# A second layer's modulation vectors computed by GpSimd products and ScalarE row sums instead of TensorE matmuls

## What is computed

```python
def modulation(cond, w, b):                       # w is 1024 x 3072
    m = jax.nn.silu(cond) @ w + b
    return jnp.split(m, 3, axis=-1)

for l in range(DEPTH):                            # DEPTH = 2
    sh, sc, gt = modulation(c, ada_w[l], ada_b[l])
    shc, scc, gtc = modulation(c_ctx, ada_w[l], ada_b[l])
    h  = rms_norm(x,  norm_pre[l]) * (1.0 + sc[:, None]) + sh[:, None]
    hc = rms_norm(xc, norm_pre[l]) * (1.0 + scc) + shc
    ...
```

## Time and profile before

| what | value |
|---|---|
| median of 3 runs | 2044.37 us |
| the profiled execution | 2042.73 us, span 2040.9 us, mean granted clock 0.986 |
| TensorE matmul busy | 1960.0 us (96%) |
| VectorE busy | 1296.8 us (64%) |
| ScalarE busy | 978.1 us (48%) |
| GpSimd busy | 30.3 us (1%), 23 instructions |
| DMA | 351.84 MB, mean 172 GB/s |

### The profile page before, as it was taken

How to read it: one execution, slowest core, us unless ns; L and a number is a source line. 1 busy time by engine, 2 the same in 40 slices (tenths; PEclk the granted TensorE clock), 3 DMA queues, 4 the chain that set the end, 5 groups by cost and what they waited for, 6 DMA issues and landing times.

```text
span 2040.9 us, 29528 instructions
## 1 busy us (share of the span) xinstructions
PE 1960.0 (96%) x12558; PEld 1702.9 (83%) x12558; DVE 1296.8 (64%) x1748; ACT 978.1 (48%) x1457; POOL 30.3 (1%) x23
## 2 busy tenths in 40 slices
PE   7799999999999999999989999999999999989998
PEld 3699999899888889999878887678888888768887
DVE  3877756878645778865565565755557555676555
ACT  1355445465334546534454445554445444565444
POOL 1300000000000000000000000000000000000000
PEclk8899999999999999999999999999999999999999
DMA  7544555434676533455445554355555555525554
GB/s 307 194 155 145 163 180 170 149 125 135 212 252 229 195 128 129 144 188 181 161 140 191 186 166 161 109 167 189 189 175 178 193 186 186 176 73 176 186 187 143
DMA packets 95410, 351.84 MB, mean 172 GB/s; under 512 B 10608, under 2 KB 10736, under 8 KB 94768
## 3 DMA queue, kind: packets, MB, share of 16 engines
q1 hardware_dynamic: 94032, 341.08, 50.6%
q0 software_dynamic: 960, 7.37, 0.9%
q10 hardware_dynamic: 288, 1.51, 0.2%
HBM read 348.87 MB, written 1.05 MB: 171 GB/s over the span
## 4 chain that ended last, share of the span: by engine, by line
PE 83%; DVE 11%; ACT 3%; DMA 2%; issue 1%; SPq 0%; DVEq 0%; ACTq 0%
PE PS L551 25%; PE PS L553 24%; PE PS L552 24%; DVE w_lo L1805 3%; DMA raw<-weights 2%; ACT w_hi L1293 1%; PE PS L629 1%; PE PS L723 1%; PE PS L954 1%; PE PS L742 1%; PE PS L917 1%; PE PS L1036 1%; PE PS L806 1%; PE PS L732 0%; PE PS L1047 0%
## 5 line engine op out<-in xcount | busy, mean ns | idle before, releaser
L1805 DVE TENSOR_TENSOR w_lo<-raw,w_hi 128x1024 fp32r<-128x1024 f32 x600 | 733.2, 1232 | 400.4 <-ACT w_hi L1293 399.0
L1293 ACT ACTIVATE w_hi<-raw 128x1024 fp32r<-128x1024 f32 x600 | 624.8, 1055 | 409.4 <-DMA raw<-weights 404.7
L551 PE MATMUL PS<-h_hi,w_hi 128*128 128x256 f32 x1568 | 455.3, 290 | 14.5 <-DVE h_lo L1823 5.4
L552 PE MATMUL PS<-h_lo,w_hi 128*128 128x256 f32 x1568 | 445.2, 284 | 0.0
L553 PE MATMUL PS<-h_hi,w_lo 128*128 128x256 f32 x1568 | 445.1, 284 | 0.0
L551 PE MATMUL PS<-w_hi,h_hi 128*128 128x512 f32 (+1 forms) x1024 | 389.2, 380 | 8.7 <-DVE h_lo L2171 6.5
L553 PE MATMUL PS<-w_hi,h_lo 128*128 128x512 f32 (+1 forms) x1024 | 380.7, 372 | 0.0
L552 PE MATMUL PS<-w_lo,h_hi 128*128 128x512 f32 (+1 forms) x1024 | 379.4, 370 | 0.0
L551 PEld LDWEIGHTS PS<-h_hi,w_hi 128*128 128x128 f32 x1568 | 302.1, 193 | 33.1 <-issue 18.9
L552 PEld LDWEIGHTS PS<-h_lo,w_hi 128*128 128x128 f32 x1568 | 302.4, 193 | 0.6 <-issue 0.5
L553 PEld LDWEIGHTS PS<-h_hi,w_lo 128*128 128x128 f32 x1568 | 302.2, 193 | 0.0
(11 more groups left out here) (256 smaller groups left out, 1855.0 us busy)
## 6 DMA issues: line engine op xcount, KB each, us to landing
raw<-weights SPq DMA_DIRECT2D x642, 512.0 KB, 3.4
x<-weights SPq DMA_DIRECT2D x6, 512.0 KB, 10.2
layer<-layer_in POOLq DMA_DIRECT2D x2, 1536.0 KB, 11.4
cx<-ctx_in POOLq DMA_DIRECT2D x1, 1024.0 KB, 8.5
x<-x_in POOLq DMA_DIRECT2D x1, 1024.0 KB, 12.5
out<-arena SPq DMA_DIRECT2D x4, 256.0 KB, 2.0
consts<-consts_in POOLq DMA_DIRECT2D x1, 928.0 KB, 9.2
arena<-filter_consts_in ACTq DMA_DIRECT2D x1, 896.0 KB, 8.3
```

The source lines that it names most:

```text
L551: pe.matmul(dst, hi, m_hi_, start=first, stop=False, **kw)
L552: pe.matmul(dst, hi, m_lo_, start=False, stop=False, **kw)
L1293: nc.scalar.activation(w_hi[:, r, :], raw[:, r, :], ACT.Copy).then_inc(w_hi_ready, 1)
L1805: V.tensor_tensor(w_lo[:, r, :], raw[:, r, :], f32(w_hi[:, r, :]), ALU.subtract).then_inc(w_lo_ready, 1)
```

## The change

- Layer 1's modulation leaves TensorE, PSUM and the ring. Its weights lie in DRAM transposed, a slot holding 128 output columns on the partitions and their 1024 weights along the row.
- A new input `cond_in` holds both condition vectors, copied to all 128 partitions (1 MB). GpSimd's queue loads it, ScalarE applies SiLU to it (`cond_silu`, behind the splits of `keys_queries`' last projection pair), and this happens twice, once in pass 0 and once in pass 1, because the memory (`beside`, in `g_hi` and `g_lo`) is used by each pass's merge stage.
- For each of the 24 slots GpSimd's queue loads the weights into one of two buffers, GpSimd makes two products of 128 x 1024 (weights by the token row, weights by the context row), and ScalarE sums each product along its row (`ada_row`: a Copy with an accumulator). There are two product buffers: a product waits until the row before last was summed.
- Pass 0's attention takes 8 slots (16 products, 2 row sums a step), pass 1's takes 16 (32 products, 4 row sums a step). The row sums stand right behind `take_turned` in each step.
- Pass 1's merge stage becomes like that of passes 0 and 2: 36 slots, no `ada`, no `ada_turn`, no copies of rows.
- VectorE's first write of `g_hi` in each of the two passes waits for the pass's row sums; `mod_vectors(1)` waits for all of them.

```diff
+            def load_ada(n):
+                pool.dma_start(ada_w[:, n % 2, :], weights[dram_pass[1] - ADA_SLOTS + n]).then_inc(ada_w_loaded[n % 2], 16)
+
+            def modulation_rows(part_):
+
+                first, end = ADA_ENDS[part_], ADA_ENDS[part_ + 1]
+                pool.wait_ge(spec_pair, DEPTH)
+                pool.dma_start(cond_rows[:, :, :], cond_in).then_inc(cond_loaded, 16)
+                load_ada(first)
+                load_ada(first + 1)
+
+                def product(i):
+                    n, w = divmod(i, 2)
+                    if i >= 2:
+                        pool.wait_ge(ada_sum, i - 1)
+                    nc.gpsimd.tensor_tensor(ada_prod[:, w, :], ada_w[:, n % 2, :], cond_rows[:, w, :],
+                                            ALU.mult).then_inc(ada_prod_ready, 1)
+
+                for n in range(first, end):
+                    if n == first:
+                        pool.wait_ge(cond_rows_act, part_ + 1)
+                    pool.wait_ge(ada_w_loaded[n % 2], 16 * (n // 2 + 1))
+                    product(2 * n)
+                    product(2 * n + 1)
+                    if n + 2 < end:
+                        pool.wait_ge(ada_prod_ready, 2 * n + 2)
+                        load_ada(n + 2)
+
+            modulation_rows(0)
+            pool.wait_ge(w_used, start["pass1"])
+            modulation_rows(1)
...
-                        if p == 1:
-                            ada(c, b, 0, i)
-                            c += 1
...
+            def cond_silu(part_):
+
+                act.wait_ge(cond_loaded, 16 * (part_ + 1))
+                nc.scalar.activation(cond_rows[:, :, :], cond_rows[:, :, :], ACT.Silu).then_inc(cond_rows_act, 1)
+
+            def ada_row(i):
+
+                act.wait_ge(ada_prod_ready, i + 1)
+                nc.scalar.activation(ada_prod[:, i % 2, :], ada_prod[:, i % 2, :], ACT.Copy,
+                                     accum_out=ada_sums[:, i:i + 1]).then_inc(ada_sum, 1)
...
                     splits(c0 + part["v"] + 2 + 2 * n)
                     take_turned(p, n)
+                    if p == 0:
+                        ada_rows_behind(p, 2 * n, 2 * n + 2)
+                    else:
+                        ada_rows_behind(p, 4 * n, 4 * n + 4)
...
+                    if p < 2 and (b, j) == (0, 0):
+                        dve.wait_ge(ada_sum, 2 * ADA_ENDS[p + 1])
```

More of the change, by code:

```diff
@@ L84, in places, with build @@
     return out, at
-def build(nc, weights, x_in, ctx_in, cols_in, consts_in, filter_consts_in, layer_in, filter_in, lam_in, tail_in, out):
+def build(nc, weights, x_in, ctx_in, cond_in, cols_in, consts_in, filter_consts_in, layer_in, filter_in, lam_in, tail_in, out):
     col_at, ncols = places(COLUMNS)
@@ L110, in build @@
     stretch("pass0", dram_pass[0], PASS_SLOTS)
[L111 to L113 removed]
+    stretch("pass1", dram_pass[0], PASS_SLOTS)
     stretch("ctx_k", dram_pass[1], 2)
@@ L118, in build @@
     dram = dram_pass[1] + PASS_SLOTS
-    for p in (0, 2):
+    for p in range(3):
         start[f"pass{p}_merge"] = start[f"pass{p}"] + MERGE_AT
@@ L154, in build @@
         taps1 = nc.alloc_sbuf_tensor_at("taps1", [P, 6, 2, BR], F32, offset=g_at)
+        beside = nc.alloc_sbuf_tensor_at("beside", [P, 6, SLOT], F32, offset=g_at)
+        cond_rows, ada_w, ada_prod = (beside[:, 2 * j:2 * j + 2, :] for j in range(3))
         qk = sb("qk", [P, 2 * KD, T])
@@ L300, in build @@
         ada_used = sem("ada_used")
+        cond_loaded = sem("cond_loaded")
+        cond_rows_act = sem("cond_rows_act")
+        ada_w_loaded = [sem(f"ada_w_loaded{j}") for j in range(2)]
+        ada_prod_ready = sem("ada_prod_ready")
+        ada_sum = sem("ada_sum")
         raw_loaded = [sem(f"raw_loaded{r}") for r in range(RING)]
@@ L413, in build @@
         block = ctx.enter_context(nc.Block())
-        def is_ada(c):
-            n = c - start["pass1_merge"]
-            return 0 <= n < MERGE_SLOTS + ADA_SLOTS and n % 5 in (0, 2)
-        def splits_to(c):
-            return c + 1 - sum(is_ada(a) for a in range(start["pass1_merge"], min(c + 1, start["pass1_wo"])))
         def f32(ap):
@@ L845, in run_pass @@
                 pe.wait_ge(act_evac, act_pairs(p, 9))
-                each = 5 if p == 1 else 3
                 for i in range(4):
                     for b in range(3):
-                        c = start[f"pass{p}_merge"] + each * (3 * i + b)
-                        if p == 1:
-                            ada(c, b, 0, i)
-                            c += 1
+                        c = start[f"pass{p}_merge"] + 3 * (3 * i + b)
                         pe.wait_ge(merge_free, i * 3 + (15 * p + b + 1))
@@ L1417, in take_turned, with ada_rows_behind @@
                                      ACT.Copy).then_inc(mixw_t_ready, 1)
+            def cond_silu(part_):
[5 more added lines that the diff above has]
+                                     accum_out=ada_sums[:, i:i + 1]).then_inc(ada_sum, 1)
+            def ada_rows_behind(p, first, end):
+                if p < 2:
+                    for i in range(2 * ADA_ENDS[p] + first, 2 * ADA_ENDS[p] + end):
+                        ada_row(i)
             def keys_queries(p, behind_second=None, src=None, event=None):
@@ L1479, in run_pass @@
                 gates("gc", 2)
-                each = 5 if p == 1 else 3
                 for i in range(4):
                     for b in range(3):
-                        c = start[f"pass{p}_merge"] + each * (3 * i + b)
-                        for j in range(-1, each - 1):
+                        c = start[f"pass{p}_merge"] + 3 * (3 * i + b)
+                        for j in range(-1, 2):
                             split(c + j + AHEAD)
                         act.wait_ge(merge_free, i * 3 + (15 * p + b + 1))
-                        act.wait_ge(w_used, c + each)
+                        act.wait_ge(w_used, c + 3)
                         nc.scalar.activation(sel[:, b, :], PS[:, 2 * b + 1, :], ACT.Sigmoid).then_inc(sel_ready, 1)
@@ L2113, in run_pass @@
                 V.memset(signal[:, 1:2], 0.0).then_inc(merge_free, 1)
-                each = 5 if p == 1 else 3
                 for i in range(4):
                     for b in range(3):
-                        c = start[f"pass{p}_merge"] + each * (3 * i + b)
-                        for j in range(-1, each - 1):
+                        c = start[f"pass{p}_merge"] + 3 * (3 * i + b)
+                        for j in range(-1, 2):
                             split(c + j + AHEAD)
-                            if p == 1 and j == 2:
-                                ada_piece(c + 1, ADA_TURNS + i, b, (6, 7))
                         dve.wait_ge(sel_ready, i * 3 + (12 * p + b + 1))
@@ L2642, in pack @@
     for l in range(DEPTH):
-        token(g["ada_w"][l])
+        if l == 0:
+            token(g["ada_w"][l])
+        else:
+            for c in range(0, 3 * D, P):
+                slots.append(g["ada_w"][l][:, c:c + P].T)
         w = g["w_in"][l]
```

68 lines of the change are left out of this document (21 added, 47 removed).

## The result

| what | before | after |
|---|---|---|
| median | 2044.12 us of 4 runs (2042.70 to 2047.22) | 2080.86 us of 4 runs (2080.00 to 2084.89) |
| ratio of the two | | 1.0185, 95% interval 1.0172 to 1.0198 |
| profiled execution | 2042.73 us, granted clock 0.986 | 2084.89 us, granted clock 0.973 |

The change costs 36.7 us.

What follows compares the result with a forecast made beforehand. TensorE's work, 83% of the span, was taken as the bound. Pass 1's merge stage -22, its attention +38 and pass 0's attention +6 gave +22 us, hence 2066 us, range 2049 to 2084.

Steps and rivals of the forecast that it cites:

- rival 4: Pass 1: GpSimd held up twice a step, +52 instead of +38, or merge stage not shrinking; 2080 us and above, chance 0.10.
- What goes, -22.1: Pass 1's merge stage: without the 24 modulation slots it takes as long as pass 0's, 22.1 us less.
- Pass 1's attention, +38: Pass 1's attention: the loop lengthens a step from 8.35 to 13.5 us, 38 us more, bounds +28 and +52.
- The 2 us added for the products that meet VectorE: Ahead of pass 1's attention: 2 us for two products meeting VectorE's busy end of `keys_queries` and for SiLU.
- What holds the mix: Pass 1's attention: GpSimd and VectorE take turns whole, so the mix gets in at 11.6 us after the turn, not 10.2.
- The bound without it: Pass 1's attention: if the mix never waits for GpSimd, a step takes 12.3 us, +28 in all.
- Splits: Both attentions: VectorE's splits take above 1.2 us, held by GpSimd's operations.
- Pass 0, +6: Pass 0's attention: +4 over eight steps of 7.7 us and +2 ahead of it, together +6, between 0 and 11.
- The opening: Ahead of pass 0's attention: `cond_in` lands at 103 to 107 us and delays the first exponential, taken as +2.
- Rival 1: Both attentions: only the handover costs, the mix is not held up; +28 and +1, 2051 us, chance 0.12.
- Rival 2: Pass 1's attention and first slots after: TensorE's clock falls too, +8 on the forecast, 2074 us, chance 0.17.
- Rival 3: Both attentions: GpSimd is quick enough, products under about 1.8 us, +11 in pass 1, 0 in pass 0; 2033 us, chance 0.05.

Runs made afterwards that it cites:

- The experiment with fills: The changed kernel with each GpSimd product replaced by three fills that read nothing and take about as long: 2059.24 us, ratio 1.0068 to before.
- the kernel with the sums first: The changed kernel with each step's row sums ahead of `take_turned` instead of behind it: 2083.52 us, ratio 1.0195 to before.
- the fillers: The changed kernel with 32 extra matmuls ahead of each turn of pass 1's attention from step 1 on: 2076.26 us, ratio 1.0152 to before.
- the last kernel: The changed kernel with 12 slots in each merge stage of passes 0 and 1, products on VectorE, row sums one step later: 2023.67 us.
- tiny sums: The changed kernel with ScalarE's row sums of 8 columns in place of 1024, products whole: 2075.46 us.

## Why the prediction was right, and where its sizes were not

- **The direction and the range** held: 2066 was predicted with 2049 to 2084, 2080.9 came. But the time lies outside the forecast's own band of 2058 to 2071, which had the chance 0.53, near the upper end of the range, where rival 4 stood with 0.10. The sum was 14.9 us short, and in the traces the terms of what comes are 16.1 short: 11.6 in pass 1 and 4.5 in pass 0.
- **What goes, -22.1**: measured -22.09, with a merge step of 8.64 us as in pass 0. That the copies out of PSUM were hidden, and that the ring keeps up, held too.
- **Pass 1's attention, +38**: measured +4.3 in the opening and +45.3 behind it, 49.6, near the upper bound of 52. The loop was the one worked out, and its first part came nearly as computed: exponentials 8.74 us after the turn, where the terms give 8.55. Behind them two sizes were off, which makes the step 14.36 instead of 13.5. The issue of a load costs GpSimd a wait of 0.30 with its 0.59, where I had 0.57: the mix was let in 12.08 us after the turn and not 11.6. The turn was put at 0.6 and took 0.94 in the mean of seven, up to 1.12. The closing was not counted at all: the last step's sums wait for products like all others, and the last gate comes 68.0 us behind the last turn instead of 64.9, 3.1 us.
- **The 2 us added for the products that meet VectorE** on the way into pass 1 were 4.3: not splits were held but the two operations of the post-norm at 399 and 402, 4.2 us together, and behind them `w_lo`, for which TensorE stood still 6.37 us, where it was 2.21 before.
- **What holds the mix.** I had bounded it by whether the mix waits, and took turns held whole. They are: what waited was not the two wide operations but the product of 128 x 1 ahead of them, and it waited for the rest of GpSimd's product. The experiment with fills put the price of the interface at about 21.6 us over both passes. The bound without it was 12.3 us a step; 13.1 came in the mean, mostly 13.25: there `tensor_scalar` was still held, and the clock was 0.90. The page "SBUF — State Buffer" of the Trainium skill (section "SBUF: two separate sides") limits the rule for two SBUF inputs to GpSimd operations that read SBUF, and a two-port mode has no such limit in it: the rows of the fills agree with both (0.16 for the tiny product, 1.00 for a `tensor_scalar` of 0.48).
- **Splits.** I expected VectorE's splits above 1.2 us in both attentions. In the steps of both two take 2.35 as before. In pass 1, GpSimd waits for a row sum at that time (no product runs from 448.2 to 452.4), and in pass 0 the splits fall almost wholly between two pairs of products (143.51 to 145.86; products end at 142.80 and begin at 145.70). In the kernel with the sums first they took 7.33, so it is the phase that spares them.
- **Pass 0, +6**: measured +10.5. The steps are 7.71 us from 136.42 on. That is the predicted length by another loop: the splits were not held, and what closes is turn taken, first row sum, two products (145.70 to 150.50), tiny product (held until 150.52), mix, turn. The seven steps between the eight turns cost 5.3 more than before; 1.1 had been gained from the first exponential to the first turn. The first step was 9.75, and there it was the clock. TensorE waited 3.25 us for the turn, the granted clock was 0.50 from 118 to 124 us, and the next turn waited for nothing but TensorE's own slots:

```profile
118.28 0.69 PE L737 MATMUL PS<-consts,arena 128*128 128x128 f32 x2 [3.25 <-DVE arena L1976]
...
128.35 0.38 PE L737 MATMUL PS<-consts,arena 128*128 128x128 f32 x2
```

The opening was put at +2 and was +6.3, 0.76 of it there already when GpSimd's last sums of the spectrum begin. I let `cond_in` alone decide, and it was there in time (SiLU waited for nothing; the two loads of `cond_in` took 6.2 us in the median, where I had 8.5 to 12.5); the ring's slot was late, by 7.24 us of ScalarE's wait, beside `cond_in` and two loads of weights. Moving these two loads gave 5.5 us back at that place.
- **The rivals.** Rival 1 (only the handover) falls: with the hold on two-input operations taken away, the kernel gains 21.6 us. Rival 2, the clock, did happen, 0.88 in the stretch; it was priced at 8 us. In pass 1 the fillers bring back 4.6 by the medians, of which only 0.9 shows in the attention; in pass 0's first step it cost about 2 (9.75 against 7.71), which the rival had not seen. The rule of the page "TensorE: Matmul & The Clock Gate" of the Trainium skill (section "HAM oscillation — how this bites in real kernels"), that waits between bursts bring the clock down in every round, is nearly what the trace shows: it fell at or behind six of the seven turns (1.11 us for a turn of 0.60) and stayed at 1.00 behind one. Its price in pass 1's steps is small, since most of the slow work has time. Rival 3 needed products of 1.8 us; GpSimd's are 2.35 undisturbed. Rival 4's first form, the mix held longer, is the nearest to the time that came, though by several small sizes and not by one more product. Its 2080 us are met by these sizes and not by its mechanism.

What stays open: how the 21.6 us between after and the kernel with fills divides between the mix, the post-norm and the splits beyond the three stretches given; and how much of the 57 us between after and the last kernel is the place and how much the engine. In the order in which I changed them, the place alone (still GpSimd) gave 27.9, the engine there 18.9 and the later sums 10.4, but no run puts VectorE's products into the attentions or GpSimd's into the merge stages with the sums one step later.

## What to carry to other kernels

Work that leaves the busiest engine is not free where the engines that take it are part of a loop that closes in each step; write that loop out, with every handover and every queued instruction, before choosing the place. An operation on GpSimd can be paid twice: with its own duration, and with the wait of a VectorE operation that comes while it runs, however small. In these traces that was so for operations with two inputs in SBUF and for `tensor_scalar`, and not for the conv, which reads PSUM (four in 1.78 us beside a product, as before). The same 48 products cost 60 us in the attentions on GpSimd and 3 us on VectorE in the merge stages, once each sum stood where its engine was waiting anyway.

## What the runs showed of the hardware that was not expected

- A VectorE product of one element a partition, 0.16 us alone, took 1.32 to 1.39 us in six steps of pass 1 and 2.87 in one, and with tiny sums 2.24 and once 3.72, until GpSimd had finished its operation; the duration of what is held says nothing of its own size.
- GpSimd fills, which read nothing, let a VectorE operation with two SBUF inputs pass (0.16, and splits at 2.35 for two), but held `tensor_scalar` of one input: 1.00 instead of 0.48 us for 128 x 512, and up to 1.04 instead of 0.17 for 128 x 2.
- The same product of 128 x 1024 takes GpSimd 2.35 to 2.4 us and VectorE 1.2.
- A GpSimd DMA issue behind a product costs 0.9 us of its time: 0.30 of wait for the product's own end and 0.59.
- Loads of 1.0 and two of 0.5 MB asked for on GpSimd's queue within 2 us delayed a slot on SyncE's ring by 4.7 us (a split at 104.00 instead of 98.50, less 0.76 of start); the load of 1.0 MB alone delayed it by 1.8 (a split at 99.80, with a start 0.46 earlier).
- TensorE's granted clock fell to 0.50 for 6 us behind a wait of 3.25 us in pass 0, and stayed at 1.00 behind one of 3.19 us in pass 1. The step with those 6 us took about 2 us more than those behind it.
